# The normalised rows on their way into the next projection: high and low parts behind each tile's turn, the weight split behind the first sum, turns one tile ahead

## The chip, the cores and the metric

The kernel runs on one NeuronCore of a Trainium2 chip. The metric is device time in microseconds (us) of one execution; of the kernel before there are three runs, with a median of 2542.18 us (2539.55 to 2543.75). The profile is of one further execution. Engines: PE is TensorE (matrix products; PEld its weight loads), DVE is VectorE, ACT is ScalarE, POOL is GpSimd, SP issues most DMAs.

## The reference, cut to what matters

The model is two layers of a first network (an even and an odd one) and one block of a second, over 512 tokens of width 1024, everything in float32. What lies around the change is this (cut):

```python
def even_layer(h, mem_n, g, w_in, ...):
    ...
    return h + (y @ w_out).astype(h.dtype)          # y: 512 x 2048, w_out: 2048 x 1024

def odd_layer(h, mem_n, g, w_in, ...):
    u = rmsnorm(h, g)
    q, kc, vc, ks, vs, kw, vw, gl, xq, gate = split_cols(u @ w_in, ODD_SPLITS)   # w_in: 1024 x 5668
    ...
    return h + (y @ w_out).astype(h.dtype)

    ...
    x = rmsnorm(h, final_g)                          # end of the first network
    h = rmsnorm(x, mix_norm_g)                       # start of the second
    z = h @ w_in                                     # 1024 x 3072
```

with `rmsnorm(x, g) = x * rsqrt(mean(x*x) + eps) * g`. At the end stands a mixture of 64 experts, each with three 1024 x 512 matrices.

So there are two places where an output projection is followed at once by a norm and an input projection: even layer to odd layer, with one norm between, and odd layer to the second network, with two norms between (`final_g`, then `mix_norm_g`).

## The kernel before

The program is a row of stages, each written out per engine; the engines meet through semaphores alone, and each engine runs its own list in order. Tokens are cut into four tiles of 128 rows (`NT = 4`).

**Products in parts.** A float32 product is made of three products of fp32r numbers: each operand is split into a high part (a cast) and a low part (the operand minus its high part). For weights ACT makes the high part (`scalar_split`, line 432), DVE the low part (`vector_split`, line 437), from a buffer `w_raw` that SP fills piece by piece (512 rows by up to 512 columns). Two pieces are held at a time. SP loads piece n only after piece n-2 was split; ACT splits piece n only after PE has done with piece n-2.

**A joined projection.** `out_projection` (line 1351) is the output projection of a layer and, in the same stretch, the norm and the first weight piece of the following input projection. It has 8 weight pieces: two blocks of 512 columns by four pieces of 512 rows. Within the last piece PE (line 1408) makes the four tiles' results one after the other, 12 products of 512 columns each; DVE adds each to the residual `h` (`add`, line 1439). The second block lies in PSUM banks 4 to 7. Before the tail, ACT and DVE split piece 0 of the next projection (`k.next_pr`, lines 1422 and 1446).

**The tail** is the class `TileNorm`. Per tile t and norm i:

- `scalar_norm(t, i)` on ACT: Square with a running sum (line 586), then Sqrt (line 589).
- `vector_scale(t)` on DVE, only with two norms: the first norm in place, reciprocal (line 622) and a product with the row of gains (line 624).
- `vector_norm(t)` on DVE: reciprocal (line 630) and product (line 636) into one of two buffers.
- `tensor(t)` on PE: a turn, 8 transposes (line 687) into two PSUM banks, 4 and 5 for even tiles, 6 and 7 for odd ones; then a wait for the tile's low part.
- `scalar_high(t)` on ACT: the high part of the turned tile, two casts (line 595).
- `vector_low(t)` on DVE: the low part, two subtractions (line 643).

After `tensor(t)` PE makes the tile's 12 products with piece 0 of the next projection (line 470, in `SplitProjection.tensor`, where `arrive(t)` calls `tail.tensor(pe, t)`), and goes on to the next tile. After the fourth tile come piece 1 and the rest of the projection.

`self.double` is true where there are two norms (the second place). The order of calls in `TileNorm.scalar` and `TileNorm.vector` is written out by hand, once for each case. The first place lies at 501 to 535 us of the span, the second at 1111 to 1155 us.

Of the kernel before, what the change touches and what calls it, by code (L numbers as in the profile page):

```python
# [8 lines left out]
ACT = mybir.ActivationFunctionType  # L9
# [8 lines left out]
NT = S // P  # L18
# [534 lines left out]
class TileNorm:  # L553
# [43 lines left out]
    def scalar(self, act):  # L597
        act.wait_ge(self.eps_set, 1)
        if self.double:
            self.scalar_norm(act, 0, 0)  # L600
            self.scalar_norm(act, 0, 1)
            self.scalar_norm(act, 1, 0)
            self.scalar_norm(act, 1, 1)
            self.scalar_norm(act, 2, 0)
            self.scalar_high(act, 0)
            self.scalar_norm(act, 3, 0)
            self.scalar_norm(act, 2, 1)
            self.scalar_high(act, 1)
            self.scalar_norm(act, 3, 1)
        else:  # L610
            self.scalar_norm(act, 0, 0)
            self.scalar_norm(act, 1, 0)
            self.scalar_norm(act, 2, 0)
            self.scalar_high(act, 0)
            self.scalar_norm(act, 3, 0)
            self.scalar_high(act, 1)
        self.scalar_high(act, 2)
        self.scalar_high(act, 3)

    def vector_scale(self, dve, t):  # L620
        dve.wait_ge(self.rooted, self.count(t, 0))
# [20 lines left out]
            dst = [self.k.u_parts[:, i, 4 * j:4 * j + 4, t * P:(t + 1) * P] for i in range(2)]  # L642
            dve.tensor_tensor(dst[1], self.bank(t, j), dst[0].bitcast(F32), ALU.subtract).then_inc(self.low, 1)  # L643

    def vector(self, dve, add):
        if self.double:
            add(0)
            self.vector_scale(dve, 0)
            add(1)
            self.vector_norm(dve, 0)  # L650
            add(2)
            self.vector_scale(dve, 1)
            add(3)
            self.vector_low(dve, 0)
            self.vector_norm(dve, 1)
            self.vector_scale(dve, 2)
            self.vector_low(dve, 1)
            self.vector_norm(dve, 2)
            self.vector_scale(dve, 3)
            self.vector_low(dve, 2)  # L660
            self.vector_norm(dve, 3)
            self.vector_low(dve, 3)
        else:
            add(0)
            add(1)
            self.vector_norm(dve, 0)
            add(2)
            self.vector_norm(dve, 1)
            add(3)
            self.vector_low(dve, 0)  # L670
            self.vector_norm(dve, 2)
            self.vector_low(dve, 1)
            self.vector_norm(dve, 3)
            self.vector_low(dve, 2)
            self.vector_low(dve, 3)
# [3 lines left out]

    def tensor(self, pe, t):  # L680

        if t < 2:
            pe.wait_ge(self.added, NT + 2 * t + 2)
        pe.wait_ge(self.gained, t + 1)
        for j in range(2):
            for kk in range(4):
                tr = pe.transpose(self.bank(t, j)[:, kk, :], self.normed[t % 2][:, (4 * j + kk) * P:(4 * j + kk + 1) * P],
                                  self.k.ident)
            tr.then_inc(self.turned, 1)
        pe.wait_ge(self.low, 2 * (t + 1))  # L690


PREP = C0 + 224
# [658 lines left out]
def out_projection(k, name, w_out, h_dram, spill, gains, table=False):  # L1352
# [21 lines left out]
    with k.block() as block:  # L1374
        @block.sync
        def _(sp):
            pr.sync(sp)
            sp.wait_ge(turned, KI)
            tail.sync(sp)

        @block.gpsimd
        def _(pool):
            pool.dma_start(h, h_dram.rearrange("(m p) n -> p m n", p=P)).then_inc(loaded, 16)
            if table:
                read_out_table(k, pool, tab_in, tab_step)
            if spill is not None:
                pool.wait_ge(added, NT * D // 512)
                pool.dma_start(spill.rearrange("(m p) n -> p m n", p=P), h).then_inc(spilled, 16)

        @block.tensor  # L1390
        def _(pe):
            for kk in range(KI):
                if kk >= 8:
                    pe.wait_ge(low, kk - 3)
                for m in range(NT):
                    t = pe.transpose(k.ps[:, turned_bank(kk), m * P:(m + 1) * P], y[:, m, kk * P:(kk + 1) * P],
                                     k.ident)
                t.then_inc(turned, 1)
            for g in pr.groups:
                if g.t == 0:  # L1400
                    pe.wait_ge(pr.low, g.n + 1)
                    if g.block == 0:
                        pe.wait_ge(low, HALF * (g.part + 1))
                w = [pr.part(g.n, i) for i in range(2)]
                for kk in range(HALF):
                    ky = HALF * (g.part % 2) + kk
                    for x, z in ((0, 0), (0, 1), (1, 0)):
                        mm = pe.matmul(k.ps[:, g.bank, :], parts[g.part // 2][:, x, ky, g.t * P:(g.t + 1) * P],  # L1408
                                       w[z][:, kk, :], start=g.part == 0 and kk == 0 and x + z == 0,
                                       stop=g.ends and kk == HALF - 1 and x == 1)  # L1410
                mm.then_inc(pr.group_done, 1)

        @block.scalar
        def _(act):
            for kk in range(KI):
                act.wait_ge(turned, kk + 1)
                act.copy(parts[kk // KD][:, 0, kk % KD, :], k.ps[:, turned_bank(kk), :]).then_inc(high, 1)
                if kk in (KD - 1, KI - 1):
                    pr.scalar_split(act, kk // KD)
            for n in range(2, len(pr.table)):  # L1420
                pr.scalar_split(act, n)
            k.next_pr.scalar_split(act, 0)
            tail.scalar(act)

        @block.vector
        def _(dve):
            for kk in range(KI):
                dve.wait_ge(high, kk + 1)
                dve.tensor_tensor(parts[kk // KD][:, 1, kk % KD, :], k.ps[:, turned_bank(kk), :],
                                  parts[kk // KD][:, 0, kk % KD, :].bitcast(F32), ALU.subtract).then_inc(low, 1)  # L1430
                if kk in (KD - 1, KI - 1):
                    pr.vector_split(dve, kk // KD)
            dve.wait_ge(loaded, 16)
            dve.memset(tail.eps, EPS).then_inc(tail.eps_set, 1)

            def add(g):
                pr.wait_group(dve, g)
                hs = h[:, g.t, 512 * g.block:512 * (g.block + 1)]
                dve.tensor_tensor(hs, hs, k.ps[:, g.bank, :], ALU.add).then_inc(added, 1)

            for g in pr.groups[:-NT]:
                if g.t == 0 and g.n:
                    pr.vector_split(dve, g.n + 1)
                if g.ends:
                    add(g)
            k.next_pr.vector_split(dve, 0)
            tail.vector(dve, lambda t: add(pr.groups[t - NT]))

# [1661 lines left out]
```

## Time and profile before

| | |
|---|---|
| median of 3 runs | 2542.18 us (2539.55 to 2543.75) |
| the profiled execution, its own time | 2539.97 us |
| its span | 2538.2 us |
| PE busy | 2252.7 us (89%) |
| DVE busy | 790.0 us (31%) |
| ACT busy | 473.9 us (19%) |
| mean granted TensorE clock | 0.96 |

The span is what the profile covers; the execution's own time is 1.8 us longer. Busy shares are averages over stages with different limits. The timeline shows instructions in order of time, neighbours of the same line merged; in square brackets stands how long the engine had been idle before and what ended that. The waits list per engine and line how long it was idle until whom. The windows give the busy time of PE, PEld, DVE, ACT and POOL in a stretch, in this order, and the mean granted clock (1.00 is 2.4 GHz, 0.50 is 1.2 GHz).

### The profile page before, as it was taken

What the parts mean: (1) busy time and instruction counts of PE and PEld (TensorE: products, weight loads), DVE (VectorE), ACT (ScalarE), POOL (GpSimd) and SP (SyncE); (2) the same over time, 40 slices, a digit from 0 to 9 for tenths busy, and PEclk for the clock granted to TensorE, in tenths of its full rate; (3) what the DMA queues carried; (4) which work ended last, traced back from release to release, by engine and by line L of the source; (5) the groups of instructions that cost most, each with busy time, mean ns of one, the idle gap of its engine ahead of it and who ended that gap; (6) DMA issues with size and microseconds to landing.
All of it is one profiled execution on the core that took longest, in us unless ns stands there. A gap on an engine that the chain in (4) does not pass through costs nothing. (4 is left out here: it accounts for less than half of the span.)

```text
span 2538.2 us, 31791 instructions
## 1 busy us (share of the span) xinstructions
PE 2252.7 (89%) x13520; PEld 1642.5 (65%) x13520; DVE 790.0 (31%) x1616; ACT 473.9 (19%) x836; POOL 201.8 (8%) x171
## 2 busy tenths in 40 slices
PE   8899978999997998889988989988998888888884
PEld 6788867878885777777874446555555555555552
DVE  7453156243310777444243221111111121111102
ACT  2222213231220444232221030000000000000001
POOL 0810000000000000650000010000000000000001
PEclk9999989999997999999998999999999999999997
DMA  9443113232315000425263447999999999999996
GB/s 284 170 133 100 57 39 113 98 113 75 126 51 154 14 22 14 167 92 184 73 119 117 140 162 316 424 425 427 426 427 425 426 426 426 425 427 426 426 427 265
DMA packets 141650, 581.43 MB, mean 229 GB/s; under 512 B 27682, under 2 KB 50326, under 8 KB 107670
## 3 DMA queue, kind: packets, MB, share of 16 engines
q1 hardware_dynamic: 127219, 428.32, 44.6%
q0 software_dynamic: 13136, 146.84, 14.0%
q10 hardware_dynamic: 1152, 4.19, 0.5%
q8 instruction: 110, 1.80, 0.3%
q14 instruction: 33, 0.27, 0.0%
HBM read 541.50 MB, written 37.63 MB: 228 GB/s over the span
## 5 line engine op out<-in xcount | busy, mean ns | idle before, releaser
L470 PE MATMUL ps<-w_parts,u_parts 128*128 128x512 f32 (+3 forms) x2016 | 429.4, 374 | 22.2 <-DVE u_parts L643 15.5
L470 PEld LDWEIGHTS ps<-w_parts,u_parts 128*128 128x128 f32 x2016 | 365.2, 190 | 82.1 <-DVE u_parts L643 17.2
L2710 PE MATMUL ps<-mem,mem_u 128*64 128x256 f32 x2880 | 347.0, 396 | 73.0 <-DMA mem<-in_expert_w_up 66.9
L2710 PEld LDWEIGHTS ps<-mem,mem_u 128*64 128x64 f32 x2880 | 225.9, 142 | 198.2 <-issue 106.2
L437 DVE TENSOR_TENSOR w_parts<-w_raw,w_parts 128x2048 fp32r<-128x2048 f32 (+3 forms) x76 | 172.7, 2273 | 409.0 <-ACT w_parts L432 409.0
L2795 DVE TENSOR_TENSOR mem_c<-mem_c,ps 128x256 f32<-128x256 f32 x64 | 27.0, 421 | 743.1 <-issue 651.8
L432 ACT CAST w_parts<-w_raw 128x2048 fp32r<-128x2048 f32 (+3 forms) x76 | 135.0, 1776 | 470.7 <-PE ps L470 193.3
L2710 PE MATMUL ps<-mem_u 128*64 128x256 f32 x1216 | 150.8, 404 | 29.8 <-DMA mem_u<-in_expert_w_up 26.8
L468 PE MATMUL ps<-u_parts,w_parts 128*128 128x512 f32 x768 | 175.3, 389 | 0.0
L1408 PE MATMUL ps<-w_parts,u_parts 128*128 128x512 f32 x768 | 175.2, 390 | 0.0
L2723 PE MATMUL ps<-mem,mem_c 128*64 128x512 f32 x736 | 166.0, 593 | 3.8 <-DMA mem<-in_expert_w_down 3.3
L1408 PEld LDWEIGHTS ps<-w_parts,u_parts 128*128 128x128 f32 x768 | 144.5, 188 | 30.0
L468 PEld LDWEIGHTS ps<-u_parts,w_parts 128*128 128x128 f32 x768 | 144.0, 188 | 29.9 <-issue 0.2
L2764 ACT ACTIVATE mem_c<-ps 128x256 f32<-128x256 f32 x64 | 24.6, 384 | 710.2 <-PE ps L2710 710.2
L2710 PEld LDWEIGHTS ps<-mem_u 128*64 128x64 f32 x1216 | 97.1, 145 | 84.9 <-issue 45.0
L2702 PEld LDWEIGHTS ps<-picks,hn_parts 128*128 128x128 f32 x1024 | 127.4, 192 | 25.3 <-issue 23.1
L2702 PE MATMUL ps<-picks,hn_parts 128*128 128x256 f32 x1024 | 140.2, 291 | 2.0 <-DVE picks L2775 2.0
L2723 PEld LDWEIGHTS ps<-mem,mem_c 128*64 128x64 f32 x736 | 53.3, 137 | 89.9 <-issue 83.7
L1774 PEld LDWEIGHTS ps<-mem_u 128*128 128x128 f32 x480 | 59.0, 191 | 30.2 <-ACT mem_u L1829 24.2
L1774 PE MATMUL ps<-mem_u 128*128 128x128 f32 x480 | 63.5, 279 | 15.8 <-ACT mem_u L1829 15.8
L2783 DVE COPY mem_u<-ps 128x512 f32<-128x512 f32 x64 | 44.3, 692 | 103.7 <-PE ps L2702 103.7
L2758 ACT COPY mem_u<-ps 128x512 f32<-128x512 f32 x64 | 37.4, 585 | 206.0 <-PE ps L2723 206.0
(373 smaller groups left out, 2226.3 us busy)
## 6 DMA issues: line engine op xcount, KB each, us to landing
mem<-in_expert_w_down SPq DMA_DIRECT2D x46, 2048.0 KB, 35.3
mem<-in_expert_w_up SPq DMA_DIRECT2D x45, 2048.0 KB, 36.1
mem<-in_expert_w_gate POOLq DMA_DIRECT2D x43, 2048.0 KB, 14.0
mem_u<-in_expert_w_up SPq DMA_DIRECT2D x19, 2048.0 KB, 35.7
mem_u<-in_expert_w_down SPq DMA_DIRECT2D x18, 2048.0 KB, 35.5
mem_u<-in_expert_w_gate POOLq DMA_DIRECT2D x18, 2048.0 KB, 14.0
w_raw<-in_od_w_in SPq DMA_DIRECT2D x18, 1024.0 KB, 4.9
ypad<-mem_u SPq DMA_DIRECT2D x128, 128.0 KB, 30.4
```

Of the source, the lines that this page charges most:

```text
L432: act.copy(self.part(n, 0), self.raw(n)).then_inc(self.high, 1)
L437: dve.tensor_tensor(self.part(n, 1), self.raw(n), self.part(n, 0).bitcast(F32), ALU.subtract).then_inc(self.low, 1)
L468: mm = pe.matmul(out, w[x][:, kk, g.t * P:(g.t + 1) * P], u[:, y, ku, :], start=first, stop=last)
L470: mm = pe.matmul(out, u[:, x, ku, g.t * P:(g.t + 1) * P], w[y][:, kk, :], start=first, stop=last)
L1408: mm = pe.matmul(k.ps[:, g.bank, :], parts[g.part // 2][:, x, ky, g.t * P:(g.t + 1) * P], w[z][:, kk, :], start=g.part == 0 and kk == 0 an ...
L1774: mm = pe.matmul(o[:, 128 * i:128 * i + 128], pT[v % 2][:, 512 * i + kt * P:512 * i + kt * P + P], vv[:, kt, g * DH:(g + 1) * DH], start=k ...
L2702: mm = pe.matmul(o, k.hn_parts[:, part, m, 2 * r + j, :], k.picks[:, q % 2, m, :, :], start=m + part == 0, stop=m == NT - 1 and part == 1)
L2710: mm = pe.matmul(ps[SLOTS * h:SLOTS * (h + 1), bank, 0:256], x[:, kk, :], w[:, kk, 256 * h:256 * (h + 1)], start=kk == 0, stop=kk == KD - 1)
L2723: mm = pe.matmul(ps[SLOTS * c:SLOTS * (c + 1), ROWS + e % 2, :], aT[:, e % 2, j, SLOTS * h:SLOTS * (h + 1)], w[:, h, j, 512 * c:512 * (c + ...
L2758: act.copy(yn[:, e % STORES, :], ps[:, ROWS + e % 2, :]).then_inc(rows_ready, 1)
L2783: dve.tensor_copy(xT[:, q % 2, 2 * r:2 * r + 2, :], ps[:, GATHER + piece % 2, :] .rearrange("p (j s) -> p j s", j=2)).then_inc(x_ready, 1)
L2795: dve.tensor_tensor(a[:, e % 2, :], sg[:, e % 2, :], ps[:, UP, 0:256], ALU.mult).then_inc(a_ready, 1)
```

## The change

Three lists are reordered and one instruction is added at each place:

1. With two norms, `scalar_high(t)` stands right behind what tile t's turn needs, and `vector_low(0)` before the last `add`.
2. In `TileNorm.vector`, the low part of the next projection's piece 0 (`vector_split(0)`, called `between`) stands behind the first `add` and no longer before it. This holds at both places.
3. With one norm, PE turns tile t+1 before it waits for tile t's low part; so each turn but the first stands one tile ahead.
4. ACT takes a Sqrt of a single number per partition before it splits that piece, at both places; the result is overwritten later.

```diff
@@ TileNorm.scalar @@
             self.scalar_norm(act, 0, 0)
             self.scalar_norm(act, 0, 1)
             self.scalar_norm(act, 1, 0)
+            self.scalar_high(act, 0)
             self.scalar_norm(act, 1, 1)
             self.scalar_norm(act, 2, 0)
-            self.scalar_high(act, 0)
             self.scalar_norm(act, 3, 0)
+            self.scalar_high(act, 1)
             self.scalar_norm(act, 2, 1)
-            self.scalar_high(act, 1)
+            self.scalar_high(act, 2)
             self.scalar_norm(act, 3, 1)
+            self.scalar_high(act, 3)
         else:
...
@@ TileNorm.vector @@
-    def vector(self, dve, add):
+    def vector(self, dve, add, between):
         if self.double:
             add(0)
+            between()
             self.vector_scale(dve, 0)
             add(1)
             self.vector_norm(dve, 0)
             add(2)
             self.vector_scale(dve, 1)
+            self.vector_low(dve, 0)
             add(3)
-            self.vector_low(dve, 0)
             self.vector_norm(dve, 1)
...
         else:
             add(0)
+            between()
             add(1)
             self.vector_norm(dve, 0)
...
@@ TileNorm.tensor @@
     def tensor(self, pe, t):
 
+        if self.double or t == 0:
+            self.turn(pe, t)
+        if not self.double and t + 1 < NT:
+            self.turn(pe, t + 1)
+        pe.wait_ge(self.low, 2 * (t + 1))
+
+    def turn(self, pe, t):
+
         if t < 2:
             pe.wait_ge(self.added, NT + 2 * t + 2)
         pe.wait_ge(self.gained, t + 1)
...
-        pe.wait_ge(self.low, 2 * (t + 1))
@@ out_projection, scalar @@
             for n in range(2, len(pr.table)):
                 pr.scalar_split(act, n)
+            act.wait_ge(tail.eps_set, 1)
+            act.activation(tail.sd[0][:, 0:1], tail.eps, ACT.Sqrt, scale=1.0, bias=tail.eps)
             k.next_pr.scalar_split(act, 0)
             tail.scalar(act)
@@ out_projection, vector @@
-            k.next_pr.vector_split(dve, 0)
-            tail.vector(dve, lambda t: add(pr.groups[t - NT]))
+            tail.vector(dve, lambda t: add(pr.groups[t - NT]), lambda: k.next_pr.vector_split(dve, 0))
```

Where the order moves, engine by engine (line numbers of the changed kernel are up to 13 higher: its turn is L699, its add L1452, its low part L645):

PE at the first place, where the odd layer's projection begins (turns of 8 transposes out of `mem`, products out of `w_parts` and `u_parts`). Before:

```order
L687 MATMUL ps<-mem_c,mem 128x128 x8
L470 MATMUL ps<-w_parts,u_parts 128x512 x12
L687 MATMUL ps<-mem_c,mem 128x128 x8
L470 MATMUL ps<-w_parts,u_parts 128x512 x12
L687 MATMUL ps<-mem_c,mem 128x128 x8
L470 MATMUL ps<-w_parts,u_parts 128x512 x12
L687 MATMUL ps<-mem_c,mem 128x128 x8
L1480 MATMUL ps<-mem_c,mem_u 128x64
L470 MATMUL ps<-w_parts,u_parts 128x512 x60
```

Now:

```order
L699 MATMUL ps<-mem_c,mem 128x128 x16
L470 MATMUL ps<-w_parts,u_parts 128x512 x12
L699 MATMUL ps<-mem_c,mem 128x128 x8
L470 MATMUL ps<-w_parts,u_parts 128x512 x12
L699 MATMUL ps<-mem_c,mem 128x128 x8
L470 MATMUL ps<-w_parts,u_parts 128x512 x12
L1492 MATMUL ps<-mem_c,mem_u 128x64
L470 MATMUL ps<-w_parts,u_parts 128x512 x60
```

Two tiles are turned before the first tile's products, and the last tile's products have no turn right before them.

ACT at the second place, in the tail with two norms (L586 and L589 are `scalar_norm`, L595 is `scalar_high`, L432 the high part of a weight piece). Before:

```order
L589 ACTIVATE mem_c<-mem_c 128x1
L586 ACTIVATE mem,mem_c<-mem 128x1024
L589 ACTIVATE mem_c<-mem_c 128x1
L586 ACTIVATE mem,mem_c<-mem 128x1024
L589 ACTIVATE mem_c<-mem_c 128x1
L586 ACTIVATE mem,mem_c<-mem 128x1024
L589 ACTIVATE mem_c<-mem_c 128x1
L595 CAST u_parts<-ps 128x4x128 x2
L586 ACTIVATE mem,mem_c<-mem 128x1024
L589 ACTIVATE mem_c<-mem_c 128x1
```

Now, from the added Sqrt on (L1434):

```order
L1434 ACT_TABLE_LOAD
L1434 ACTIVATE mem_c<-mem_c 128x1
L432 CAST w_parts<-w_raw 128x2048
L586 ACTIVATE mem,mem_c<-mem 128x1024
L589 ACTIVATE mem_c<-mem_c 128x1
L586 ACTIVATE mem,mem_c<-mem 128x1024
L589 ACTIVATE mem_c<-mem_c 128x1
L586 ACTIVATE mem,mem_c<-mem 128x1024
L589 ACTIVATE mem_c<-mem_c 128x1
L595 CAST u_parts<-ps 128x4x128 x2
L586 ACTIVATE mem,mem_c<-mem 128x1024
L589 ACTIVATE mem_c<-mem_c 128x1
```

Tile 0's high part stood behind five norms and now stands behind three; the table load that stood at the first norm now stands before the split.

DVE at the second place (L437 is the low part of a weight piece, four of which in a row were three of the projection before and piece 0 of the next). Before:

```order
L437 TENSOR_TENSOR w_parts<-w_raw,w_parts 128x2048 x4
L1439 TENSOR_TENSOR mem<-mem,ps 128x512
L622 RECIPROCAL mem_c<-mem_c 128x1
L624 SCALAR_TENSOR_TENSOR mem<-mem,mem_c 128x1024
L1439 TENSOR_TENSOR mem<-mem,ps 128x512
L630 RECIPROCAL mem_c<-mem_c 128x1
L636 SCALAR_TENSOR_TENSOR mem<-mem,mem_c 128x1024
L1439 TENSOR_TENSOR mem<-mem,ps 128x512
L622 RECIPROCAL mem_c<-mem_c 128x1
L624 SCALAR_TENSOR_TENSOR mem<-mem,mem_c 128x1024
L1439 TENSOR_TENSOR mem<-mem,ps 128x512
L643 TENSOR_TENSOR u_parts<-ps,u_parts 128x4x128 x2
```

Now:

```order
L1452 TENSOR_TENSOR mem<-mem,ps 128x512
L437 TENSOR_TENSOR w_parts<-w_raw,w_parts 128x2048
L624 RECIPROCAL mem_c<-mem_c 128x1
L626 SCALAR_TENSOR_TENSOR mem<-mem,mem_c 128x1024
L1452 TENSOR_TENSOR mem<-mem,ps 128x512
L632 RECIPROCAL mem_c<-mem_c 128x1
L638 SCALAR_TENSOR_TENSOR mem<-mem,mem_c 128x1024
L1452 TENSOR_TENSOR mem<-mem,ps 128x512
L624 RECIPROCAL mem_c<-mem_c 128x1
L626 SCALAR_TENSOR_TENSOR mem<-mem,mem_c 128x1024
L645 TENSOR_TENSOR u_parts<-ps,u_parts 128x4x128 x2
L1452 TENSOR_TENSOR mem<-mem,ps 128x512
```

The split of piece 0 moved behind the first add, tile 0's low part before the fourth.

## Rows read from the trace of the kernel before

**Rows 1.** The page: the chain of work that ended last, share of the span by engine.

```profile
DMA 27%; PE 11%; DVE 1%; issue 0%; ACT 0%; POOL 0%; SPq 0%; DVEq 0%; POOLq 0%
```

**Rows 2.** Windows at the experts: us, busy per engine (instructions), PEclk, DMA share, GB/s.

```profile
1520.00:1560.00 40.00, 33.64 (x243) 25.62 (x244) 10.72 (x28) 3.17 (x7) 0.57 (x1) 0.87 0.62 253
1560.00:2500.00 940.00, 831.66 (x6012) 517.22 (x6013) 116.60 (x256) 60.06 (x124) 31.67 (x60) 0.97 1.01 424
```

**Rows 3.** Waits of PE, 500 to 560 us: us in total, times, longest.

```profile
PE ps L470 <- DVE u_parts L643: 4.7, 3, 1.6
PE ps L1480 <- DVE u_parts L643: 1.6, 1, 1.6
```

**Rows 4.** Waits of PE, 1110 to 1160 us.

```profile
PE ps L470 <- DVE u_parts L643: 10.8, 4, 5.5
PE ps L687 <- DVE mem L636: 1.6, 1, 1.6
PE ps L470 <- DVE w_parts L437: 0.2, 1, 0.2
```

**Rows 5.** Timeline of PE, first place: start us, us, instructions, [idle before].

```profile
504.75 7.42 PE L1408 MATMUL ps<-w_parts,u_parts 128*128 128x512 f32 x32
512.01 1.03 PE L687 MATMUL ps<-mem_c,mem 128*128 128x128 f32 x8
514.61 3.02 PE L470 MATMUL ps<-w_parts,u_parts 128*128 128x512 f32 x12 [1.56 <-DVE u_parts L643]
517.47 1.04 PE L687 MATMUL ps<-mem_c,mem 128*128 128x128 f32 x8
```

**Rows 6.** Timeline of the other engines, first place.

```profile
505.54 0.68 DVE L1439 TENSOR_TENSOR mem<-mem,ps 128x512 f32<-128x512 f32 x1
...
507.48 1.28 ACT L589 ACT_TABLE_LOAD   x1
...
513.27 1.29 DVE L643 TENSOR_TENSOR u_parts<-ps,u_parts 128x512 fp32r<-128x512 f32 x2
...
514.66 1.29 DVE L636 SCALAR_TENSOR_TENSOR mem<-mem,mem_c 128x1024 f32<-128x1024 f32 x1
...
534.28 10.75 PEld L470 LDWEIGHTS ps<-w_parts,u_parts 128*128 128x128 f32 x48 [0.50 <-DVE w_parts L437]
```

**Rows 7.** Timeline of PE, second place.

```profile
1109.68 12.85 PE L1408 MATMUL ps<-w_parts,u_parts 128*128 128x512 f32 x56
1124.12 1.07 PE L687 MATMUL ps<-mem_c,mem 128*128 128x128 f32 x8 [1.59 <-DVE mem L636]
1130.69 4.91 PE L470 MATMUL ps<-w_parts,u_parts 128*128 128x512 f32 x12 [5.50 <-DVE u_parts L643]
...
1144.13 4.61 PE L470 MATMUL ps<-w_parts,u_parts 128*128 128x512 f32 x12 [2.19 <-DVE u_parts L643]
...
1151.18 3.07 PE L470 MATMUL ps<-w_parts,u_parts 128*128 128x512 f32 x12 [1.56 <-DVE u_parts L643]
1154.47 5.76 PE L470 MATMUL ps<-w_parts,u_parts 128*128 128x512 f32 x24 [0.22 <-DVE w_parts L437]
```

**Rows 8.** Timeline of DVE and ACT, second place.

```profile
1113.70 2.29 DVE L437 TENSOR_TENSOR w_parts<-w_raw,w_parts 128x2048 fp32r<-128x2048 f32 x1 [8.25 <-ACT w_parts L432]
...
1119.67 1.28 DVE L624 SCALAR_TENSOR_TENSOR mem<-mem,mem_c 128x1024 f32<-128x1024 f32 x1
...
1120.99 1.06 ACT L586 ACTIVATE mem<-mem 128x1024 f32<-128x1024 f32 x1 [1.55 <-DVE mem L624]
...
1122.17 0.29 ACT L589 ACTIVATE mem_c<-mem_c 128x1 f32<-128x1 f32 x1
...
1128.75 1.05 ACT L595 CAST u_parts<-ps 128x512 fp32r<-128x512 f32 x2
```

**Rows 9.** Windows of half a microsecond, second place, columns as in rows 2.

```profile
1130.50:1131.00 0.50, 0.30 (x1) 0.31 (x2) 0.46 (x3) 0.47 (x3) 0.00 (x0) 0.50 0.00 0
1145.50:1146.00 0.50, 0.50 (x2) 0.40 (x2) 0.00 (x0) 0.00 (x0) 0.00 (x0) 0.50 1.04 410
```

More of the change, by code:

```diff
@@ L616, in scalar @@
             self.scalar_high(act, 1)
-        self.scalar_high(act, 2)
-        self.scalar_high(act, 3)
+            self.scalar_high(act, 2)
+            self.scalar_high(act, 3)
     def vector_scale(self, dve, t):
```

## The prediction

> **What bounds the kernel now.** I read the page's chain of work first. What ended last is, by engine, a DMA 27% of the span [rows 1], and the windows say where: from 1560 us on the DMA engines are full, 424 GB/s for 940 us, while the experts' weights stream in; in the 40 us before they are at 0.62 [rows 2]. So the end is bound by a stream that begins when the stages before it are done. Those stages are bound by PE: what shortens them moves the stream forward whole, if nothing else starts it.
>
> Then I read PE's waits in the two joined projections. At the first place PE waits for the low parts of the turned tiles (DVE L643) four times, 1.6 us each, 6.3 us in all [rows 3]. At the second it waits 10.8 us for them in four waits, the longest 5.5 us, and 1.6 us for the first normed tile [rows 4]. The timeline shows the pattern: a turn of 8 transposes, 1.03 us; 1.56 us of idleness, in which ACT makes the high part and DVE the low part; then the tile's 12 products, 2.86 us from their start to the next turn's [rows 5]. A tile thus takes 1.03 + 1.56 + 2.86 = 5.45 us, the distance from 514.61 to the next tile's products.
>
> **First place, one norm.** The projection before ends its last products at 504.75 + 7.42 = 512.17 us [rows 5], one tile's 12 products every 2.73 us before that, so tile 0's sum could be added from 512.17 - 3 x 2.73 = 503.98. It was added at 505.54 [rows 6], behind the weight split. Afterwards: add(0) 504.0 to 504.7, split to 507.0 (2.29 as in [rows 8]), add(1) to 507.7. The root needs a Square and a Sqrt, 1.47 us from the start of one to the end of the other [rows 8]: at 506.3 now, since the table load of 1.28 us that stood between them [rows 6] lies in the time in which ACT waits for PE before the split. Tile 0 is normed by 509.2. This gains nothing at PE: the turn starts at 512.01 in the trace, directly behind the products, and still will. The second turn needs the fourth add; with it done at about 512.9 and tile 1 normed at 511.6, PE makes it from 513.05 to 514.1, in the time in which it was idle. Tile 0's products start at 514.5, as before (514.61), because high and low part of tile 0 take as long as before (low part from 513.27, 1.29 us [rows 6]). From below the first place could lose here, too: PE waits in its order for the second turn, with tile 0's products behind it, and each microsecond that the fourth add or tile 1's norm were later than 513 would come on top.
>
> From there the three waits of 1.56 us and their like fall: PE makes 12 products (2.73), turn (1.03), 12 products, turn, 12 products, a small transpose (0.2), 12 products: 4 x 2.73 + 2 x 1.03 + 0.2 = 13.2, so it stands before piece 1 at 527.7. Checked on the other engines: norm(2) on DVE is done at 516.0 (its row took 1.29 [rows 6]), PE wants it at 517.4; tile 1's low part is done at 517.3, wanted at 518.3; tile 2's at 520.1, wanted at 522; tile 3's at 523.3, wanted at 524.9. Piece 1's split follows tile 3's parts on ACT and DVE; at the second place it ended 3.3 us behind the low part (1151.18 to 1154.47 [rows 7]), so it is done by 526.7. Before, piece 1's first weight load was at 534.28 [rows 6]. **Gain 6.6 us.** Counted the other way: three of four waits, 3 x 1.56 = 4.7; the second turn, 1.03, which now lies in the wait that stays; 0.5 us of waiting for piece 1's split (the bracket in [rows 6]); together 6.2, the rest being weight loads that now overlap. From below it is the 4.7 alone; from above, if the fourth wait went too, 7.8. I take the timeline's 6.6.
>
> **Second place, two norms.** The projection before ends at 1109.68 + 12.85 = 1122.53 [rows 7], so tile 0 can be added at 1114.4. Before, the split (1113.70, 2.29 us [rows 8]) held it until 1115.9, and the scaling of tile 0 started at 1119.67 [rows 8]. Now: add(0) to 1115.1; split to 1117.4; the root is ready at 1116.7 without the table load; scaling's product 1117.55 to 1118.8; ACT's Square follows the product's start by 1.32 (1119.67 to 1120.99), the root takes 1.47, DVE's reciprocal and product some 1.5 after it, so tile 0 is normed at 1121.9. PE is free at 1122.5 and turns it 1122.4 to 1123.4; before, it waited 1.59 us for it, until 1124.12 [rows 7].
>
> Then the largest term. Before, the high part started at 1128.75 [rows 8] though the turn had ended at 1125.19: ACT had two norms of the next tiles ahead of it, one of them waiting for DVE. Now ACT makes it at once, 1123.0 to 1124.1 (1.05 [rows 8]), DVE has the scaling of tile 1 behind it at 1123.9 and makes the low part to 1125.1. Tile 0's products start at 1125.2 instead of 1130.69 [rows 7]: 5.5 us.
>
> The steps after it: tile 1 is normed at 1127.1 and wanted at 1127.8; tile 2 at 1132.7, wanted at 1133.3; tile 3 at 1138.1, wanted at 1138.7. DVE and ACT keep ahead of PE by 0.6 us, so each tile takes the 5.45 us of the first place: tile 3's products start at 1125.2 + 16.4 = 1141.6. Piece 1 starts 3.3 us later, at 1144.9, because the split sits behind tile 3's parts as before (0.22 us of waiting [rows 7]). Before it started at 1154.47 [rows 7]: **gain 9.6 us**. In it are 1.9 and 1.6 us that come from the clock: the 12 products of tiles 0 and 2 took 4.91 and 4.61 us [rows 7] against 3.02 [rows 5], and in both stretches the granted clock was 0.50, that is 1.2 of 2.4 GHz [rows 9]. It fell within the idleness of 5.50 us, and again behind one of 2.19 us [rows 7]. At the first place, with four of 1.56 us, it stayed whole, so I count on a whole clock where idleness is 1.6 to 1.8 us.
>
> Of the added Sqrt (some 0.3 us and the table load) nothing lies on the path: ACT's split waits for PE, long enough that DVE behind it had been idle for 8.25 us [rows 8]; without that cover it would cost 0.3 to 1.6 us. The later split delays SP's load of piece 2 by 1.4 us, which has until the end of piece 0, ten microseconds later. POOL's copies of `h` follow adds or scalings that come earlier.
>
> **The sum.** 6.6 + 9.6 = 16.2 us. The profiled execution took 2539.97 us and would take 2523.8; it lies 2.2 us below the median of the runs, 2542.18, which gives 2526.0. About 0.2%, 5 us, is what a measurement of this kernel can tell from no change.
>
> **The rivals.**
> - *The clock stays low in part.* The trace has a fall behind idleness of 2.19 us, and 1.8 us is close to it. One group of products at 1.2 GHz costs 1.6 to 1.9 us, two 3.5: 2527.7 to 2529.5. For it: both falls are at the second place, where a turn with little other work stands between two idle stretches, which stays so. Against it: the four whole tiles of the first place. Chance 0.15. The Trainium skill (TensorE: Matmul & The Clock Gate, Part 1) has a free-running window decide, so that the same gap may or may not throttle; by that rule the clock at the second place is chance rather than settled, and the two falls of this trace, behind gaps so different, agree.
> - *DVE or ACT don't keep 0.6 us ahead* at the second place. Then PE waits for a normed tile instead of a low part, up to 1 us in each of three tiles: 2527 to 2529. For it: DVE has 4.9 us of work in 5.45 per tile (add 0.68, scaling and norm 1.45 each, low part 1.29). Chance 0.08.
> - *The turn ahead does not pay* at the first place, because something I don't see holds PE at the second turn (it waits in order, with tile 0's products behind it): only 9.6 us are left, 2532.6. Chance 0.04.
> - *The stream hides it.* If the experts' stream did not begin earlier, both gains would end there: 2542. Against it: its share is 0.62 before 1560 us [rows 2], so it is the stages that start it. Chance 0.03.
> - *Slower.* An earlier stream that runs less well: each load is issued when PE has left a buffer, and the order in which three queues' transfers meet could shift. It decides if the rate over the 940 us falls by more than 2.3%, from 424 to 414 GB/s: that is 21.6 us, 5 more than is gained, 2547. Nothing in the windows speaks for it but that it is by far the longest stretch. Chance 0.02.
>
> **How the numbers follow.** 0.68 is left for the forecast, 2526.0; its own range is 2523.5 to 2528.5 (the three runs spread over 4 us, and 1 us either way in each term). The range takes in the clock and the late DVE, and most of the case of 9.6 us: 2521.5 to 2531.5. Faster by over 0.2%: all but the last two, 0.95; within: 0.03; slower: 0.02.
>
> **What would show it.** Right: in the changed profile PE's first-place waits for L645 are one of about 1.5 us instead of four; piece 1 starts 6.6 us earlier; at the second place the first wait for the low part is 1.8 instead of 5.5 us, all four are below 1.9, the clock stays at 1.00, and the following stage starts 16 us earlier than before; the experts' stream keeps 424 GB/s. Wrong: a wait of PE on L638 (a normed tile) at either place, windows with a clock of 0.50 at the second place, a table load between the casts and the norms, or a stage further on that begins less early than the one before it.

## The result and the profile after

The changed kernel takes 2527.39 us (median of 4 runs, 2524.57 to 2529.24) against 2541.91 us of the kernel before beside it: ratio 0.9944, 95% interval 0.9928 to 0.9960. That is 14.5 us less (by the interval, 10 to 18); 16.2 were forecast. Its profiled execution is the slowest of the four, 2529.24 us with a span of 2527.4.

The waits of PE at the first place, then at the second (columns as in [rows 3]); they answer to [rows 3] and [rows 4]:

```profile
PE ps L470 <- DVE u_parts L645: 0.6, 1, 0.6
```

```profile
PE ps L470 <- DVE u_parts L645: 6.2, 4, 1.6
PE ps L470 <- DVE w_parts L437: 0.3, 1, 0.3
```

Of four waits of 1.6 us at the first place one of 0.6 is left. At the second, the 5.5 us and the 1.6 us for the normed tile are gone, and what remains is four plain waits between a turn and its products, and 0.3 us ahead of piece 1.

The timeline of PE at the first place, which answers to [rows 5]:

```profile
502.75 9.91 PE L1419 MATMUL ps<-w_parts,u_parts 128*128 128x512 f32 x43
512.50 2.03 PE L699 MATMUL ps<-mem_c,mem 128*128 128x128 f32 x16
515.10 3.02 PE L470 MATMUL ps<-w_parts,u_parts 128*128 128x512 f32 x12 [0.56 <-DVE u_parts L645]
...
518.74 2.99 PE L470 MATMUL ps<-w_parts,u_parts 128*128 128x512 f32 x12
...
522.36 3.01 PE L470 MATMUL ps<-w_parts,u_parts 128*128 128x512 f32 x12
525.30 0.27 PE L1492 MATMUL ps<-mem_c,mem_u 64*128 64x64 f32 x1
```

The turn of two tiles takes 2.03 us in one piece, and from 515.10 on there is no bracket: products and turns follow each other. Tile 0's products start 2.44 us after the end of the last products (502.75 + 9.91 = 512.66), exactly as before (514.61 - 512.17). From the first turn to the small transpose ahead of tile 3's products it is 12.80 us; before it was 530.99 - 512.01 = 18.98.

The timeline of PE at the second place, which answers to [rows 7]:

```profile
1099.75 19.66 PE L1419 MATMUL ps<-w_parts,u_parts 128*128 128x512 f32 x86
1119.25 1.03 PE L699 MATMUL ps<-mem_c,mem 128*128 128x128 f32 x8
1121.85 3.02 PE L470 MATMUL ps<-w_parts,u_parts 128*128 128x512 f32 x12 [1.56 <-DVE u_parts L645]
...
1127.31 3.03 PE L470 MATMUL ps<-w_parts,u_parts 128*128 128x512 f32 x12 [1.56 <-DVE u_parts L645]
...
1132.77 3.06 PE L470 MATMUL ps<-w_parts,u_parts 128*128 128x512 f32 x12 [1.56 <-DVE u_parts L645]
...
1138.27 3.01 PE L470 MATMUL ps<-w_parts,u_parts 128*128 128x512 f32 x12 [1.56 <-DVE u_parts L645]
1141.56 11.22 PE L470 MATMUL ps<-w_parts,u_parts 128*128 128x512 f32 x48 [0.28 <-DVE w_parts L437]
```

The last products end at 1119.41 and the turn is right behind them. Every tile's products take 3.0 us, and the granted clock is 1.00 from 1119 to 1142 us: no half clock. Piece 1 starts 22.15 us after the end of the last products; before it was 1154.47 - 1122.53 = 31.94. The other engines there, answering to [rows 8]:

```profile
1111.29 0.69 DVE L1452 TENSOR_TENSOR mem<-mem,ps 128x512 f32<-128x512 f32 x1 [8.80 <-PE ps L1419]
1111.89 2.29 DVE L437 TENSOR_TENSOR w_parts<-w_raw,w_parts 128x2048 fp32r<-128x2048 f32 x1
1112.07 1.06 ACT L586 ACTIVATE mem<-mem 128x1024 f32<-128x1024 f32 x1 [1.54 <-DVE mem L1452]
...
1114.29 1.29 DVE L626 SCALAR_TENSOR_TENSOR mem<-mem,mem_c 128x1024 f32<-128x1024 f32 x1
...
1115.61 1.06 ACT L586 ACTIVATE mem<-mem 128x1024 f32<-128x1024 f32 x1 [2.06 <-DVE mem L626]
...
1119.88 1.07 ACT L595 CAST u_parts<-ps 128x512 fp32r<-128x512 f32 x2 [1.43 <-PE ps L699]
```

The first sum stands before the weight split, the Square begins 0.78 us after the sum's start, no table load follows it, and ACT makes tile 0's high part 0.63 us after its turn began, where it had waited 4.6 (1124.12 to 1128.75).

Where the time went over the whole program is read from the first DMA that SP issues in a stage, in us of the span:

| stage | before | after | earlier by |
|---|---|---|---|
| ahead of the first place (odd layer's first piece) | 483.88 | 484.37 | -0.5 |
| compression | 766.68 | 760.63 | 6.05 |
| its table of distances is stored | 798.41 | 792.44 | 5.97 |
| attention | 810.37 | 806.74 | 3.63 |
| odd layer's output projection | 1019.16 | 1016.32 | 2.84 |
| state-space stage (behind the second place) | 1290.75 | 1277.86 | 12.89 |
| experts' first weights | 1453.47 | 1440.22 | 13.25 |
| end of the span | 2538.2 | 2527.4 | 10.8 |

So the first place gives 6.5 us and the stretch with the second 10.05 (9.8 of them in its tail), as forecast. In this pair of profiles 0.5 us are lost before the first place, 2.3 in the compression, 0.8 in the attention and 2.4 among the experts. The experiments ask what belongs to the change, part by part, and whether the losses do.

### The profile page after: what moved, and what is told of

Same layout as the page of the kernel before. It is cut to its first block and busy times, and to the rows that moved or that the text cites. A ratio compares the mean times of both kernels' runs of the same rounds, so it can differ in the third digit from the quotient of the medians.

```text
span 2527.4 us, 31793 instructions
## 1 busy us (share of the span) xinstructions
PE 2244.6 (89%) x13520; PEld 1636.1 (65%) x13520; DVE 788.5 (31%) x1616; ACT 474.6 (19%) x838; POOL 202.9 (8%) x171
## 5 line engine op out<-in xcount | busy, mean ns | idle before, releaser
L437 DVE TENSOR_TENSOR w_parts<-w_raw,w_parts 128x2048 fp32r<-128x2048 f32 (+3 forms) x76 | 171.7, 2260 | 392.9 <-ACT w_parts L432 392.9
L432 ACT CAST w_parts<-w_raw 128x2048 fp32r<-128x2048 f32 (+3 forms) x76 | 135.0, 1776 | 468.6 <-PE ps L470 194.3
```

What stands on the lines that cost most here:

```text
L432: act.copy(self.part(n, 0), self.raw(n)).then_inc(self.high, 1)
L437: dve.tensor_tensor(self.part(n, 1), self.raw(n), self.part(n, 0).bitcast(F32), ALU.subtract).then_inc(self.low, 1)
```

## The experiments

Each kernel's profile is read at the same two distances. **Distance 1**: from the first turn of the first place to the small transpose ahead of tile 3's products. **Distance 2**: from the end of the last products to the start of piece 1 at the second place. Times are medians; "before" is the kernel before, run beside each group. The distances are read from one profile of each kernel.

| kernel | us | before beside it | distance 1 | distance 2 |
|---|---|---|---|---|
| before (first profile) | 2541.91 | | 18.98 | 31.94 |
| changed (first profile) | 2527.39 | 2541.91 | 12.80 | 22.15 |
| ctl_before | 2540.01 | 2542.28 | 18.97 | 31.84 |
| ctl_after | 2523.01 | 2542.28 | 12.79 | 22.15 |
| ctl_after2 | 2527.53 | 2541.13 | 12.78 | 22.10 |
| undo_turns | 2530.67 | 2542.28 | 19.01 | 22.10 |
| undo_order | 2531.21 | 2542.28 | 12.79 | 29.37 |
| undo_split | 2524.49 (one run) | 2543.49 | 12.79 | 23.05 |
| undo_table | 2525.58 (one run) | 2543.49 | 12.82 | 22.85 |
| undo_both | 2529.09 (one run) | 2543.49 | 12.81 | 26.11 |
| half_wait | 2524.20 | 2543.49 | 12.17 | 20.62 |
| early_split | 2523.61 | 2541.13 | 12.21 | 20.35 |

The distances repeat to 0.1 us where the whole time moves by several us between runs of one kernel (before: 2537.68 to 2548.91 in 22 runs). Part of that arises before anything is changed: the last products ahead of the first place end at 510.5 to 514.3 us of the span in the twelve profiles, and ctl_after has the 510.5.

### The two kernels again: ctl_before, ctl_after, ctl_after2

No edit.

> The kernel before once more, unchanged. Theory A (the tails are all that the change touches; what was given back in the compression stage, where 64 products took 9.88 us instead of 8.42 and 8 more 1.92 instead of 1.06, is where the clock happened to fall): 2539 to 2544 us, the tails as in the trace of before to 0.1 us (piece 1 of the next projection 22.3 us behind the end of the first place's last products, 31.9 us at the second), while the 64 products of the compression may take anything from 8.4 to 9.9 us. Theory B (an earlier arrival costs the compression stage 2 to 3 us as a rule): the 64 products take 8.4 us again.

> The changed kernel once more. Theory A: 2524.5 to 2529 us, tails as in the trace of after to 0.1 us (PE waits 0.6 us at the first place, four times 1.6 us at the second), the 64 products of the compression anywhere between 8.4 and 9.9 us. Theory B: they take 9.9 us again, and the odd layer's stages give back 2 to 3 us of the first place's gain.

> The changed kernel a third time, beside early_split on the same chip. Theory A: tails as in the first two traces to 0.1 us; the 64 products of the compression 8.4 to 9.9 us, wherever the clock falls; 2521 to 2528 us, some 3 us more than early_split, which the timing may or may not tell apart.

Measured ratios to the kernel before: ctl_before 0.9993 (0.9982 to 1.0005), ctl_after 0.9931 (0.9914 to 0.9949), ctl_after2 0.9944 (0.9931 to 0.9957). The gain is thus 14.5, 19.3 and 13.6 us in three comparisons, 15.8 on average. How far such a comparison can be off is seen in ctl_before, the same kernel as the one beside it, and 2.3 us lower; against ctl_before, ctl_after gains 17.0. ctl_after's median of 2523.01 lies below its expected range, the other two lie in theirs.

The 64 products of the compression, from the timeline of PE: of the kernel before and of the changed one in the first profiles,

```profile
797.60 8.42 PE L1585 MATMUL ps<-mem 128*63 128x256 f32 x64
```

```profile
791.63 9.88 PE L1597 MATMUL ps<-mem 128*63 128x256 f32 x64
```

and in ctl_before, ctl_after and ctl_after2:

```profile
798.04 9.07 PE L1585 MATMUL ps<-mem 128*63 128x256 f32 x64
```

```profile
789.44 8.51 PE L1597 MATMUL ps<-mem 128*63 128x256 f32 x64
```

```profile
790.30 8.61 PE L1597 MATMUL ps<-mem 128*63 128x256 f32 x64
```

Theory B falls: with the change in, the same products take 9.88, 8.51 and 8.61 us, without it 8.42 and 9.07. The windows say what varies (us, busy time of PE, PEld, DVE, ACT and POOL, granted clock, DMA share, GB/s). Of before, then of the changed kernel:

```profile
797.60:806.00 8.40, 8.40 (x65) 6.29 (x64) 0.82 (x2) 0.00 (x0) 0.00 (x0) 0.84 0.10 12
808.00:810.00 2.00, 1.65 (x12) 1.31 (x12) 0.76 (x3) 0.01 (x1) 0.00 (x0) 1.00 0.00 0
```

```profile
791.63:801.50 9.87, 9.87 (x65) 6.55 (x64) 0.82 (x2) 0.00 (x0) 0.00 (x0) 0.72 0.08 10
803.50:806.10 2.60, 2.52 (x12) 1.76 (x12) 0.50 (x2) 0.00 (x1) 0.00 (x0) 0.61 0.00 0
```

The mean granted clock over these products was 0.84 in the one and 0.72 in the other, and on the small products behind them 1.00 against 0.61. This stage has idle stretches of 6 and 9 us on PE whatever the change does, and how much of the work after them runs at 1.2 GHz differs from execution to execution. The experts' part varies as well: from their first weights to the end of the span it is 1084.7 us before and 1087.2 after in the first pair, but 1084.0, 1084.4 and 1084.2 us in ctl_before, ctl_after and ctl_after2, and 1084.3 to 1085.7 in the other seven.

### The first place: undo_turns

```diff
     def tensor(self, pe, t):
-        if self.double or t == 0:
-            self.turn(pe, t)
-        if not self.double and t + 1 < NT:
-            self.turn(pe, t + 1)
+        self.turn(pe, t)
         pe.wait_ge(self.low, 2 * (t + 1))
```

> The changed kernel, but PE at the first place turns each tile only behind the products of the one before, as it did. Theory A (the turn ahead is the whole gain of the first place; the table load and the later split give nothing there, since PE is still busy when tile 0 is normed): four waits of 1.56 us are back, piece 1 starts 6.5 us later than in the changed kernel relative to the end of the last products, the second place is untouched, 2532.5 to 2535 us. Rival (the earlier norm of tile 0 and the table load give part of it): less than 5 us come back at the first place.

2530.67 us, ratio 0.9959 (0.9948 to 0.9971); 7.7 us more than ctl_after beside it, below the absolute range, as ctl_after was. PE at the first place:

```profile
512.89 1.03 PE L696 MATMUL ps<-mem_c,mem 128*128 128x128 f32 x8
515.49 3.02 PE L470 MATMUL ps<-w_parts,u_parts 128*128 128x512 f32 x12 [1.56 <-DVE u_parts L645]
...
520.95 3.06 PE L470 MATMUL ps<-w_parts,u_parts 128*128 128x512 f32 x12 [1.56 <-DVE u_parts L645]
```

Every tile again has its 1.56 us. Distance 1 is 19.01, that of before to 0.03 us, though table load and split stand where the change puts them: all 6.2 us of it come from the turns. PE's weight loads wait 0.5 us for piece 1's split again, a wait that the turns ahead had removed as well. Distance 2 is untouched. Theory A holds.

### The second place, order of the high parts: undo_order

```diff
             self.scalar_norm(act, 1, 0)
-            self.scalar_high(act, 0)
             self.scalar_norm(act, 1, 1)
             self.scalar_norm(act, 2, 0)
+            self.scalar_high(act, 0)
             self.scalar_norm(act, 3, 0)
...
             self.vector_scale(dve, 1)
-            self.vector_low(dve, 0)
             add(3)
+            self.vector_low(dve, 0)
```

(The high parts of tiles 1 to 3 go back likewise.)

> The changed kernel, but at the second place ACT's high parts and DVE's first low part stand where they stood. Theory A (the order of the high parts is the larger part of the second gain, and with it goes a half clock): tile 0's high part waits behind two more norms, so tile 0's products start 3.5 us later than in the changed kernel; PE is idle for 5.1 us before them, the granted clock falls to 0.50 again and costs 1.5 to 3.5 us more: piece 1 is 5 to 7 us later, 2532 to 2535 us. Rival (the earlier start through split and table load is most of the 9.9 us): piece 1 is less than 3.5 us later and no stretch of the tail has a clock of 0.50.

2531.21 us, ratio 0.9959 (0.9948 to 0.9969), 8.2 us above ctl_after. Distance 2 grows by 7.2 us. PE:

```profile
1116.19 1.04 PE L699 MATMUL ps<-mem_c,mem 128*128 128x128 f32 x8
1122.25 4.61 PE L470 MATMUL ps<-w_parts,u_parts 128*128 128x512 f32 x12 [5.03 <-DVE u_parts L645]
...
1132.15 1.03 PE L699 MATMUL ps<-mem_c,mem 128*128 128x128 f32 x8
1135.38 4.62 PE L470 MATMUL ps<-w_parts,u_parts 128*128 128x512 f32 x12 [2.19 <-DVE u_parts L645]
```

The first products wait 5.03 us instead of 1.56 (3.5 us, as expected) and take 4.61; the third tile's wait 2.19 and take 4.62. The windows show the half clock within both groups (the first and the third row), but a whole one through the idle stretch ahead of the third tile (the second row):

```profile
1123.00:1124.00 1.00, 1.00 (x4) 0.79 (x3) 0.96 (x3) 0.00 (x0) 0.00 (x0) 0.50 0.02 8
1133.20:1135.30 2.10, 0.00 (x0) 0.00 (x0) 1.26 (x3) 1.26 (x4) 0.00 (x0) 1.00 0.80 322
1137.00:1138.00 1.00, 1.00 (x4) 0.81 (x3) 0.00 (x0) 0.00 (x0) 0.00 (x0) 0.50 1.01 406
```

3.5 + 1.6 + 0.6 + 1.6 = 7.3 us. Theory A holds, just above its range of 5 to 7 us (the time of 2531.21 lies below its 2532 to 2535, as ctl_after lay below its own): undoing the order of the high parts and of the first low part alone takes away 7.2 of the second place's 9.8 us, and 3.2 of them are the clock.

### Split and table load: undo_split, undo_table, undo_both

```diff
-            tail.vector(dve, lambda t: add(...), lambda: k.next_pr.vector_split(dve, 0))
+            k.next_pr.vector_split(dve, 0)
+            tail.vector(dve, lambda t: add(...), lambda: None)
```

```diff
-            act.wait_ge(tail.eps_set, 1)
-            act.activation(tail.sd[0][:, 0:1], tail.eps, ACT.Sqrt, scale=1.0, bias=tail.eps)
```

undo_both has both edits.

> The changed kernel, but the low part of the next projection's piece 0 stands before the first add again. Theory A: at the first place nothing changes at PE (the turn starts with PE, which is busy until then); at the second the first scaling starts 0.7 us later, tile 0 is normed 0.7 us later and 0.2 to 0.4 us behind the end of PE's products, so piece 1 is 0.3 to 0.6 us later. Rival (the split's place is what the second place gains by): 1.5 us or more.

> The changed kernel without the added Sqrt, so the table load is back between the first Square and its Sqrt. Theory A: the root comes 1.28 us later, but DVE is in the weight split for 0.7 us of that: the first scaling is 0.6 us later at the second place, piece 1 0.1 to 0.3 us, nothing at the first place. Rival (a switch of tables costs more than its row, since the engine must also run empty): the first root is 2.6 us later and piece 1 more than 1 us.

> The changed kernel without the added Sqrt and with the split before the first add. Theory A: the two hide each other, and undone together they cost more than the sum of the two alone: the first scaling 2 us later than in the changed kernel, tile 0 turned 1.5 us later, piece 1 at the second place 1.4 to 1.7 us later; nothing at the first place. Rival (they add up): 0.4 to 0.9 us.

Distance 1 is 12.79, 12.82 and 12.81: neither part gives anything at the first place. At the second, undo_split loses 0.9 us (0.3 to 0.6 expected) and undo_table 0.7 (0.1 to 0.3). PE in undo_split:

```profile
1114.44 1.07 PE L699 MATMUL ps<-mem_c,mem 128*128 128x128 f32 x8 [0.30 <-DVE mem L638]
1117.54 3.02 PE L470 MATMUL ps<-w_parts,u_parts 128*128 128x512 f32 x12 [2.03 <-DVE u_parts L645]
```

The turn starts 0.30 us behind the end of the products, as expected (0.46 us later than in the changed kernel, where it stands 0.16 before it). But the wait behind the turn grew from 1.56 to 2.03 us, which I had not reckoned: once PE no longer holds the turn up, the chain that counts is DVE's own, where add and scaling of tile 1 stand between tile 0's norm (1113.02) and its low part (1116.21). undo_table shows the same 2.03.

In undo_both the loss is 4.0 us, more than double the expected 1.4 to 1.7:

```profile
1118.48 1.06 PE L699 MATMUL ps<-mem_c,mem 128*128 128x128 f32 x8 [1.92 <-DVE mem L638]
1121.57 4.45 PE L470 MATMUL ps<-w_parts,u_parts 128*128 128x512 f32 x12 [2.03 <-DVE u_parts L645]
```

The turn comes 2.08 us later, the wait behind it is 0.47 longer, and the products take 4.45 instead of 3.04 us, again at half clock:

```profile
1122.00:1123.00 1.00, 1.00 (x3) 0.73 (x3) 0.96 (x3) 0.97 (x3) 0.00 (x0) 0.50 0.00 0
```

So the two parts do hide each other (2.55 us without the clock, against 0.9 + 0.7). The rest is the clock: idle stretches of 1.92 and 2.03 us with a 1.06 us turn between them were enough for the clock to fall, while 2.03 us behind 0.30 in undo_split was not. These are single profiles; how often a kernel with such stretches keeps its whole clock was not measured.

### A version that waits for half: half_wait, early_split

Piece 0 of the weights holds rows 0 to 511, and so needs only the first of a tile's two halves. half_wait:

```diff
-        pe.wait_ge(self.low, 2 * (t + 1))
+        pe.wait_ge(self.low, 2 * t + 1 if self.double or t < NT - 1 else 2 * NT)
...
     def turn(self, pe, t):
+        if t >= 2:
+            pe.wait_ge(self.low, 2 * (t - 1))
...
             def guest(block, bank):
                 b = block - 1
+                if block == 0:
+                    pe.wait_ge(tail.low, 2 * NT)
```

early_split adds, at the second place, `scalar_split(act, 1)` ahead of `scalar_high(act, 3)` and `vector_split(dve, 1)` ahead of `vector_low(dve, 3)`, and takes both out of the place behind them where they stood.

> The changed kernel, but PE waits before a tile's products only for the low part of the tile's first half (piece 0 of the weights needs no more); the second half is waited for before piece 1 and before its banks are turned into again. Theory A: at the second place each period falls from 5.46 to 4.8 us (ACT and DVE can do 4.65), so tile 3's products start 0.65 + 3 x 0.65 = 2.6 us earlier; piece 1, which waits for its own split behind tile 3's parts, starts 1.9 us earlier; at the first place 0.5 us; 2.4 us in all, 0.1%, at the edge of what the timing tells. Rival (DVE is the bound there now, with 4.9 us of work per tile): PE waits for normed tiles instead, and piece 1 is less than 1 us earlier.

> half_wait, and at the second place piece 1 of the weights is split between the last norm and tile 3's parts: ACT makes its high part (1.91 us) in the 3.0 us in which it waits for tile 3's turn, DVE its low part (2.29 us) in 2.1 us of waiting. Theory A (in half_wait piece 1 waits 0.96 us for a split that stands behind tile 3's parts for no reason): PE makes piece 1 directly behind tile 3's products, at most 0.3 us of the gain going to DVE's overrun before tile 3's low part; piece 1 is 0.9 to 1.3 us earlier than in half_wait, 2.4 to 2.8 us than in the changed kernel at the second place, 3.0 to 3.4 us with the first place; some 2519 to 2523 us. Rival (the split in that place holds tile 3's high part up): piece 1 is no earlier than in half_wait.

half_wait:

```profile
1115.42 1.03 PE L701 MATMUL ps<-mem_c,mem 128*128 128x128 f32 x8
1117.42 3.06 PE L470 MATMUL ps<-w_parts,u_parts 128*128 128x512 f32 x12 [0.96 <-DVE u_parts L645]
...
1122.50 3.02 PE L470 MATMUL ps<-w_parts,u_parts 128*128 128x512 f32 x12 [1.14 <-DVE u_parts L645]
...
1127.36 3.02 PE L470 MATMUL ps<-w_parts,u_parts 128*128 128x512 f32 x12 [0.96 <-DVE u_parts L645]
...
1132.22 3.02 PE L470 MATMUL ps<-w_parts,u_parts 128*128 128x512 f32 x12 [0.97 <-DVE u_parts L645]
1136.20 11.16 PE L470 MATMUL ps<-w_parts,u_parts 128*128 128x512 f32 x48 [0.96 <-DVE w_parts L437]
```

The waits fall from 1.56 to 0.96 us (once 1.14), the distance from one tile's products to the next from 5.46 to 5.08, 4.86 and 4.86 us. Distance 1 is 0.6 us shorter, distance 2 1.5 (1.9 expected): piece 1 now waits 0.96 us for its split. Together 2.2 us. In time it is 2524.20 us (2518.34 to 2526.85), ratio 0.9924 (0.9909 to 0.9938), against 0.9944, 0.9931 and 0.9944 of the changed kernel: in the right direction, but the intervals overlap.

early_split does not hold what it promised:

```profile
1129.32 1.89 ACT L432 CAST w_parts<-w_raw 128x2048 fp32r<-128x2048 f32 x1
...
1131.25 2.29 DVE L437 TENSOR_TENSOR w_parts<-w_raw,w_parts 128x2048 fp32r<-128x2048 f32 x1 [0.32 <-ACT w_parts L432]
1131.83 1.07 ACT L595 CAST u_parts<-ps 128x512 fp32r<-128x512 f32 x2 [0.61 <-PE ps L703]
1133.46 1.28 DVE L646 TENSOR_TENSOR u_parts<-ps,u_parts 128x512 fp32r<-128x512 f32 x2
...
1134.19 3.99 PEld L470 LDWEIGHTS ps<-w_parts,u_parts 128*128 128x128 f32 x18 [2.21 <-DVE u_parts L646]
```

Piece 1 follows directly, but DVE's split could start only at 1131.25, when ACT's 1.89 us were over, and runs for 2.29, so tile 3's low part starts at 1133.46 and PE waits 1.97 us instead of 0.97. The one wait's gain is mostly eaten by the other: 0.3 us are left of the expected 0.9 to 1.3; the rival was nearer. I had taken DVE's room (2.1 us) from the changed kernel; in half_wait, whose tiles come faster, it is 1.5. Ratio 0.9929 (0.9917 to 0.9942): no better than half_wait, so half_wait is what I would keep. Beside ctl_after2 (2527.53 us, 0.9944) it is 3.9 us lower in the medians and 2.3 us shorter by the two distances, but these intervals overlap too: that the two places are shorter is shown by the distances, that the whole kernel is faster than the changed one is not shown by the times.

## Why the prediction was right

**The bound.** That the stages before the experts set the end is borne out: the experts' part takes 1084.0 to 1085.7 us in eleven of twelve profiles, whether it starts at 1453 or at 1435, so what comes earlier there ends earlier. Only the first profile of the changed kernel has 1087.2. Why is open: PE's waits for weights sum to 103.4 us in it and 97.9 in before, but 103.0 in ctl_before and 106.7 in ctl_after, which are not longer.

**First place, 6.6 us.** Distance 1 shrank by 6.2 us and the wait of 0.5 us for piece 1 went with it, in all 6.7 (6.5 by the table of stages). undo_turns shows that it is the turns alone, as the working said. That tile 0's products start no earlier or later held to 0.01 us. One figure in the list of signs contradicted the working: it said that one wait of about 1.5 us would stay, but a turn of 1.03 us had been put into it, and it measured 0.56.

**Second place, 9.6 us.** Measured 9.8. The largest term, 5.5 us, holds for the start of tile 0's products: they started 1130.69 - 1122.53 = 8.16 us behind the end of the last products, and now 1121.85 - 1119.41 = 2.44, which is 5.7 less. The working put all of it to the high part being made at once. That was too much: 1.75 us come from the turn, which started 1.59 us behind the end of the last products and now 0.16 before it, and the order of the high parts gives the other 3.94 (the wait of 5.50 is 1.56), which agrees with the 3.5 us that undo_order loses there. The rest of what undo_order loses is 3.2 us of clock and 0.6 of waiting. The equal periods of 5.46 us came as reckoned, with DVE and ACT ahead of PE by 0.6 us and a little more (tile 1's norm ends at 1123.85, the weight loads of its turn start at 1124.48 and the turn at 1124.71). Piece 1 starts 3.29 us behind tile 3's products, as assumed. The first wait, for which the list of signs had 1.8 us, measured 1.56 like the others.

**The clock.** The forecast counted on a whole clock where idleness is 1.6 to 1.8 us, and all three profiles of the changed kernel have products of 3.0 us in each tile; that rival fell. At the second place all three traces with an idle stretch of 5 us and one of 2.2 us behind it (before, ctl_before, undo_order) had both falls, so chance showed little there. But when the clock fell differed: in before at 1127.9, within the 5.50 us, in undo_order 0.3 us after the products had started. In the compression, where nothing was changed, the same 64 products took 8.3 to 9.9 us over the twelve profiles. The Trainium skill (TensorE: Matmul & The Clock Gate, Part 1) says that the window in which activity is watched is free-running, so that it depends on where in it the work lands when the clock changes. Both observations fit with that; no run here tests it.

**The 1.7 us between forecast and first result.** The interval of the first comparison, 10 to 18 us, takes in the 16.2, and over three comparisons the gain is 15.8 us, so no term is shown to be missing from the sum. That it comes as near as that is partly luck, since three gains of one pair of kernels are 13.6, 14.5 and 19.3 us; the distances, 6.2 + 0.5 and 9.8 us, are the better witness. The pair of first profiles shows what chance can do: 2.3 us in the compression and 2.4 among the experts, which did not come back in ctl_after and ctl_after2.

**What was not seen.** For the added Sqrt the forecast said only that it costs nothing, and left the gain of split and table load inside one chain. Their share is 0.7 to 0.9 us each, but 4.0 together, since either hides the other and since a half clock returns when both are missing. So the parts don't add up: order of the high parts 7.2, split and table load 4.0, against 9.8 for all. The two overlap, and in both a half clock has its share.

## What to carry to other kernels

Where an engine's list is ordered by hand, put each step right behind the one that frees it if the costliest engine waits for it, and let that engine start on the next tile before it waits for this one; look in the timeline for a finished result that nobody takes up, like the turn that ended at 1125.19 and was read at 1128.75. Idle stretches of 2 us on TensorE cost another 1.4 to 1.6 us in the products behind them where the clock fell (undo_both, before, undo_order), and nothing where it did not (undo_split), so a cut in idle time can be worth more there than its own length. And check small edits by a distance between two events in the trace: it repeats to 0.1 us where the whole time wanders by 5.

## What the hardware showed that I had not expected

- The clock fell at idle stretches far shorter than the one of 5.5 us: with 2.19 us (before, undo_order; 2.18 in ctl_before) and with 1.92 and 2.03 us around a short turn (undo_both), but not with four of 1.56 us, nor with 2.03 behind 0.30 (undo_split). Which property of the work in between decides, these runs don't settle.
- The clock can fall after the idle stretch rather than in it. In before it was granted whole through the 2.19 us (1.00 from 1141.95 to 1144.10), fell at 1145.0, 0.9 us into the products of tile 2; in undo_order it fell 0.8 us into them.
- The same stretch of the compression ran at a mean clock of 0.72 in one profile and 0.84 in another without any change near it. With the small products behind it the difference is 2.3 us, as much as many an edit.
- A table load showed only its row of 1.28 us: in undo_both the Sqrt starts at 1113.49, right behind a load from 1112.20, and DVE's reciprocal follows 0.33 us later. The Trainium skill (ScalarE: Activation LUTs, What ACT_TABLE_LOAD costs) adds some 1.38 us of draining to each switch. Here it cannot be seen: from the start of tile 0's sum to DVE's scaling it is 2.48 us in undo_split, where the Sqrt's table is loaded ahead, and 3.76 in undo_both, which is later by 1.28, the load's own row.
